# Cross-attention of eight sample tokens: which operand of the value product stays in TensorE and which is streamed

## The reference

```python
def cross_attn(h, mkv, w_q, w_o):
    B, S, _ = h.shape
    q = (h @ w_q).reshape(B, S, MEM_HEADS, MEM_HEAD_DIM)
    s = jnp.einsum('bshd,bmhd->bhsm', q, mkv[:, :, 0].astype(q.dtype)).astype(jnp.float32) * MEM_SCALE
    p = jax.nn.softmax(s, axis=-1).astype(q.dtype)
    o = jnp.einsum('bhsm,bmhd->bshd', p, mkv[:, :, 1].astype(q.dtype)).reshape(B, S, MEM_WIDTH)
    return o @ w_o
```

## Time and profile before

| | |
|---|---|
| median of 3 runs (lowest to highest) | 2244.89 us (2244.49 to 2246.28) |
| the profiled execution, its own time | 2242.0 us |
| its span, first to last instruction | 2240.3 us |
| TensorE busy | 2011.1 us, 90% of the span |
| VectorE, ScalarE, GpSimd busy | 954.0, 622.1, 124.5 us |
| mean granted clock of TensorE | 0.917 |

### The profile page before, as it was taken

The page is one execution under the profiler, slowest core; times in us unless marked ns, Lnnn a source line. Parts: engine busy times, 40 slices in busy tenths (PEclk is TensorE's granted clock), DMA queues, the critical chain, the costliest instruction groups (busy, mean ns, idle before and its releaser), DMA issues. The chain is left out here.

```text
span 2240.3 us, 29586 instructions
## 1 busy us (share of the span) xinstructions
PE 2011.1 (90%) x11972; PEld 1741.7 (78%) x11972; DVE 954.0 (43%) x2319; ACT 622.1 (28%) x1225; POOL 124.5 (6%) x204
## 2 busy tenths in 40 slices
PE   7799899778899988886989899699999999999994
PEld 5486555567888887656976776599999999999993
DVE  6837945457777555115240043423222232313236
ACT  4022111424444645322251144411111111111112
POOL 2000101211110002200000000000000000000000
PEclk9899999779999989766979798699999999999997
DMA  6050030433431009621311201011111111111102
GB/s 161 19 162 12 29 102 28 132 126 122 133 114 48 1 1 209 157 68 29 123 57 35 78 11 46 26 41 46 49 43 52 41 54 38 57 38 55 31 19 85
DMA packets 127934, 150.20 MB, mean 67 GB/s; under 512 B 12840, under 2 KB 112344, under 8 KB 121624
## 3 DMA queue, kind: packets, MB, share of 16 engines
q1 hardware_dynamic: 111592, 70.21, 10.9%
q0 software_dynamic: 14336, 72.24, 10.7%
q10 hardware_dynamic: 1872, 5.86, 0.7%
HBM read 140.17 MB, written 12.31 MB: 68 GB/s over the span
## 5 line engine op out<-in xcount | busy, mean ns | idle before, releaser
L684 PE MATMUL PS<-A 128*128 128x64 f32 (+15 forms) x3728 | 716.2, 350 | 33.9 <-issue 15.3
L684 PEld LDWEIGHTS PS<-A 128*128 128x128 f32 (+4 forms) x3728 | 523.0, 194 | 216.6 <-issue 89.3
L688 PE MATMUL PS<-ident,A 128*128 128x128 f32 (+9 forms) x1512 | 238.0, 303 | 99.5 <-ACT A L1445 33.3
L1445 ACT ACTIVATE A<-PS 128x344 f32<-128x344 f32 (+17 forms) x378 | 208.8, 570 | 406.0 <-PE PS L684 343.2
L688 PEld LDWEIGHTS PS<-ident,A 128*128 128x128 f32 (+9 forms) x1512 | 189.1, 151 | 135.3 <-issue 27.1
L1868 DVE TENSOR_TENSOR A<-A 128x16 f32<-128x16 f32 (+12 forms) x273 | 215.1, 796 | 119.9 <-ACTq L1756 109.6
L684 PE MATMUL PS<-hH,wL 128*128 128x344 f32 x1056 | 224.6, 321 | 6.1 <-issue 6.1
L684 PE MATMUL PS<-hL,wH 128*128 128x344 f32 x1056 | 224.6, 321 | 0.0
L684 PE MATMUL PS<-hH,wH 128*128 128x344 f32 x1056 | 223.7, 320 | 0.0
L684 PEld LDWEIGHTS PS<-hH,wL 128*128 128x128 f32 x1056 | 177.4, 189 | 7.3 <-issue 7.3
L1445 ACT ACTIVATE A<-A,st 128x640 f32<-128x640 f32 (+9 forms) x149 | 116.7, 784 | 223.6 <-DVE st L2301 212.2
(11 more groups left out here) (273 smaller groups left out, 1879.9 us busy)
## 6 DMA issues: line engine op xcount, KB each, us to landing
wRaw<-in_ffn_wi SPq DMA_DIRECT2D x44, 512.0 KB, 3.8
wRaw<-in_ffn_wo SPq DMA_DIRECT2D x28, 384.0 KB, 3.1
A<-in_cache_mem_kv POOLq DMA_DIRECT2D x16, 512.0 KB, 7.3
A<-in_x_prompt SPq DMA_DIRECT2D x8, 512.0 KB, 8.3
A<-in_w_in SPq DMA_DIRECT2D x8, 512.0 KB, 9.8
A<-in_xkv SPq DMA_DIRECT2D x8, 512.0 KB, 4.0
A<-bias_by_distance POOLq DMA_DIRECT2D x8, 512.0 KB, 4.0
A<-out SPq DMA_DIRECT2D x16, 256.0 KB, 5.1
```

Of the source, the lines that this page charges most:

```text
L684: return nc.tensor.matmul(out, lhsT=lhsT, rhs=rhs, start=start, stop=stop, skip_group_check=True)
L688: return nc.tensor.transpose(out, in_, ident[b:b + n, b:b + n])
L1445: return a_.activation(out, in_, func, **kw)
```

## The change

The value product of the sample turns round. The probabilities become the stationary side: `pz` holds, for each half and each token, 128 rows by 32 columns that are zero but for the token's four columns. The values move, 512 columns (all four heads) at a time, and 16 products add up into one unit of 32 rows by 512 columns. Of row 4 b + h only the 128 columns of head h are wanted. ScalarE copies the unit to `oX`, TensorE transposes it in four pieces (the new unit `xV`), and VectorE picks the wanted columns out of each. GpSimd clears `pz` once, right behind the clearing of `qxz`, in a stage that ends some 90 us before the values.

```diff
     for i in range(NT + 3):
-        order += [("XS", i)] if i < NT else []
+        order += (["xV"] if i == 2 else []) + ([("XS", i)] if i < NT else [])
...
-        PTxs = at(17440 + 256, 2, 32)
+        pz = at(17696, 2, DB, 32)
+        oX = at(16416, 512)
...
             for b in range(DB):
-                for h in range(XH):
-                    for i in range(2):
-                        ins = mm(s[:, h * DB + b:h * DB + b + 1], Vm[:, b, i, h * P:(h + 1) * P],
-                                 PTxs[:, i, b * XH + h:b * XH + h + 1], i == 0, i == 1)
+                for i in range(2):
+                    ins = mm(s[0:32, 0:512], pz[:, i, b], Vm[:, b, i], b + i == 0, b + i == DB)
...
             for i in range(NT + 3):
+                if i == 2:
+
+                    read_out(pe, "xO")
+                    s = open_("xV")
+                    for h in range(XH):
+                        ins = tr(s[:, h * 32:(h + 1) * 32], oX[0:32, h * P:(h + 1) * P])
+                    ins.then_inc(filled, 1)
...
             g.memset(qxz, 0.0).then_inc(qxz_zero, 1)
+            g.memset(pz, 0.0).then_inc(qxz_zero, 1)
...
             full(act, "xP")
-            free(f(PTxs.rearrange("p a c -> p (a c)"), slot("xP")[:, 0:64]), "xP")
+            act.wait_ge(qxz_zero, 2)
+            for h in range(XH):
+                own.step(f(pz.rearrange("p i b c -> p i (b c)")[:, :, h::36],
+                           slot("xP")[:, 0:64].rearrange("p (i b h) -> p i b h", i=2, h=XH)[:, :, :, h]))
+            own.settle()
+            act.sem_inc(emptied[U["xP"] % 4], 1)
+            full(act, "xO")
+            free(f(oX[0:32], slot("xO")[0:32, 0:512]), "xO")
...
-            full(dve, "xO")
-            free(v.tensor_copy(q2T[:, :, T:TC], slot("xO")[:, 0:32].rearrange("p (h b) -> p h b", h=XH)), "xO")
             for i in range(NT + 3):
+                if i == 2:
+
+                    full(dve, "xV")
+                    for h in range(XH):
+                        own.step(v.tensor_copy(q2T[:, h, T:TC], slot("xV")[:, 0:P].rearrange("p (h b k) -> p h b k", h=XH, k=XH)[:, h, :, h]))
+                    own.settle()
+                    dve.sem_inc(emptied[U["xV"] % 4], 1)
```

## The result

The changed kernel took 2229.8 us (median of 4 executions, 2220.52 to 2231.9), the kernel before 2245.59 us in the same comparison; the ratio is 0.9927, with a 95% interval of 0.9899 to 0.9956. That is 15.8 us less, where 11.9 was forecast; the ratio applied to the median of before gives 2228.5 us, under the low end of the range. The profiled execution had a span of 2218.8 us.

A forecast was written before the change was run, and what follows sets the result against it. The prediction took TensorE itself to bound the sample's value stage, at a granted clock of 0.50. Terms +0.4 − 11.1 − 1.5 gave −12.2 us, from 2244.9 to 2232.7, forecast 2233, range 2229.5 to 2238 us.

The forecast's parts named there:

- The handover: Sample's probabilities to the values: four strided ScalarE copies replace one and TensorE waits for the last, +0.4 us.
- The values: Sample's value product: 128 one-column records of 25.0 us become 32 records of 512 columns in 13.9 us, net −11.1 us.
- rival A: Behind the handover: one low-clock stretch of 3.2 us costs the values 1.6 us, total 2234.3 us; chance 0.27.
- The prompt's first scores: Start of prompt loop: scores at full clock, VectorE's copies add 0.5, first values 11.65 us behind the sample's, −1.5 us.
- At nothing: Result's transposes, ScalarE's copy to oX and GpSimd's clearing of pz: covered by waits or other work, no cost.
- B: Sample's values: clock stays low through the new stream, up to 28.2 us, total 2249.3 us, slower; chance 0.04.
- C: Start of prompt loop: VectorE's copies wait for xV, the −1.5 becomes +1, total 2235.5 us; chance 0.08.
- D: Sample's values are not on the chain, so nothing changes, 2245 us; chance 0.01.

The follow-up runs named there:

- again: The changed kernel run once more with no edit: 2226.39 us, ratio 0.9934 to the kernel before.
- interleaved form: Changed kernel with ScalarE's and VectorE's four copies each made one, two prompt tiles' scores moved into TensorE's waits: 2224.28 us, then 2225.04 us.
- wide: Kernel before with each of the 64 value products moving 128 columns, heads as outer loop: 2232.14 us, ratio 0.9942.
- wide32: Kernel before with each of the 64 value products moving 32 columns, heads as outer loop: 2240.52 us, ratio 0.9996.
- before_again: The kernel before run once more with no edit, for a second profile: one execution, 2246.06 us.

## Why the prediction was right and wrong

**The handover: +0.4 forecast, +0.24 measured** (0.86 against 0.62 us from the first transpose to the values). The copies cost the 0.2 us assumed: 0.42 us for all four against 0.22 for the one, so +0.20 for three more, less than the +0.32 that the prediction gave beside its own figure. The wait for the last of them, put at 0.2, cost 0.04.

**The values: 13.9 us forecast, 13.9 measured** in all three profiles without a low stretch, 15.6 in the one with it. The 1.7 us of that stretch are rival A's 1.6.

**The prompt's first scores: first values at 11.65 us behind the sample's forecast, 11.65 measured** (again: 20.80 − 13.9 to the transposes of the first tile, and 4.75 from there). The maxima moved by 0.52 us for 0.5. From there to the output projection it is 28.77 to 28.82 us in all profiles but those of the interleaved form: the same distances as before, as forecast.

**At nothing.** ScalarE's copy of the result lasts 0.59 us and ends 2.8 us ahead of its first exponentials. The transposes of the result take 0.43 us inside TensorE's wait, which is still 0.95 us. GpSimd's clearing of pz moved the first six key loads by 0.5 us, with 90 us to spare:

```profile
1129.25 0.95 POOL L1421 MEMSET A<- 128x1024 f32 x1 [159.56 <-PE PS L685]
1130.14 0.52 POOL L1422 MEMSET A<- 128x512 f32 x1
1130.61 4.26 POOL L1427 DMA_DIRECT2D A<-in_cache_mem_kv  x6
```

**Rivals.** A came true in one of four profiles. B is refuted: the streams of 512 columns hold 1.00. C and D are out by the distances above. The 128 loads behind which 128 columns move took about 14.6 us (wide: 19.74 less 24 score records at 0.213), and 25.6 behind which 32 move (wide32). The rule of the Trainium skill (TensorE: Matmul & The Clock Gate, section "LDWEIGHTS (loading the stationary operand)") that a load costs its columns divided by 1.2, in ns, would make both 13.7 us, an estimate; the first trace is near it, the second disagrees.

**What failed is the step from the stage to the whole.** The stage gave 12.4 us against the first profile of before (38.81 − 26.42), and averaged over the profiles 12.1: 38.81, 39.15 and 38.97 us of the three with the low clock (before, before_again, wide32), 28.12, 26.42, 26.42 and 26.41 of the changed kernel. The kernel gained 15.8 in the first comparison and 14.7 pooled. For all that lies outside the stage the sum has no term, for a change of the clock there or for chance; the only allowance of its kind in the range, "another 1 to 2 us either way", was for the prompt's first scores. I took the median of before from three executions that lay within 1.8 us of each other, and executions of one kernel lie anywhere in 22. Two things fell into the gap. One is chance: the first comparison had 4 executions a side, and its 15.8 is 1.1 over the pooled mean. With the pooled gain the time would be 2244.9 − 14.7 = 2230.2 us, inside the range, so the miss by 1 us is in part bad luck.

The other is what is left, 14.7 − 12.1 = 2.6 us, barely over the 2.0 that the pooled means leave open. It may be chance too. It may also be that the clock, left at 1.00 by the stage, falls less often behind it: the output projection up to the second residual took 60.46, 59.57 and 61.19 us in the three profiles with the low values and 59.56 or 59.57 in all nine others, the second residual 52.05, 50.26 and 50.54 against 50.18 to 50.51. That would be 1.4 us. The rest of the kernel gives nothing more: from the start of the FFN to the end it is 806.1 to 806.5 us in the three and 805.7 to 806.9 in the nine. Three profiles against nine can't settle it, and it stays open.

## What to carry to other kernels

Where TensorE is busy throughout and its products move one or a few columns behind each full load, look at the granted clock of that stretch before counting instructions. There the choice of the stationary side can matter by what it streams, and padding the moving side with columns that nobody reads can be worth as much as a new layout, at a fraction of the edits. The clock line shows where else to look: its slices from 952 to 1064 us show a 6, lower than the 7 of the stage that was changed, and the products with 4 moving columns lie in them. No run here tried to change those. Then judge a gain of half a per cent by the stage in two or three profiles, and not by three executions of the whole.

## What the runs showed of the hardware that was not expected

- The 128 records of 64 products with 128 by 128 stationary blocks took 25.0 and 26.0 us with 1 column moving, 25.6 with 32 and about 14.6 with 128: more streaming was faster, through the clock.
- The same program ran its attention loop (430 to 820 us) at a mean clock of 0.88 to 0.92 from one execution to the next, and two profiles of the kernel before were 11 us apart behind it. Whole executions of this kernel differ by up to 22 us.
- Four strided ScalarE copies of 16 columns out of PSUM take 0.42 us in a row, four VectorE copies of 8 columns 0.38 us.
